# Seven quarter products for eight in the up and gate units of a two-block transformer kernel

## The chip, the cores and the metric

The kernel runs on one core of one Trainium2 chip. The metric is the device time of one execution in microseconds (us). An engine is called by its name in the profile: PE (matrix products; PEld are its weight loads), DVE (VectorE), ACT (ScalarE), POOL (GpSimd) and SP (which issues the weight transfers).

## The reference, cut to what matters

Two blocks in a row work on 512 tokens of 1024 features. The first has a gated feed-forward in each of its two layers, the second a squared-ReLU one in each of its two. These four are what the change touches:

```python
def swiglu_ffn(x, w_gate, w_up, w_down):                 # first block, 2 layers, D_FF = 2816
    return (jax.nn.silu(x @ w_gate) * (x @ w_up)) @ w_down
...
def sq_relu_mlp(h, w_up, w_down):                        # second block, 2 layers, D_FF_2 = 4096
    u = jax.nn.relu(h @ w_up)
    return (u * u) @ w_down
```

All else (an HGRN2 and convolution mixer, cross attention to 256 memory tokens, a pooling mixer, gated linear attention, sliding-window attention, norms) stays as it is.

## The kernel before, in words

**Precision.** Every float32 operand is split in two fp32r parts, a high one (a copy by ACT) and a low one (the rest, a subtraction by DVE), and each product is three matmuls: high by high, low by high, high by low (`mm3`).

**Units.** The weights come as 1 MB units of 128 x 2048 (w_raw, two slots, c % 2). Of unit c, ACT makes w_hi (`split_hi`), DVE makes w_lo (`split_lo`), and SP loads unit c + 2 into the slot when w_lo of unit c is there. ACT may write w_hi of unit c when PE has used unit c - 2 (semaphore unit_used).

**Chunks.** A feed-forward is cut in chunks of 256 hidden features: 11 for ffn0 and ffn1, 16 for mlp0 and mlp1. A chunk of an ffn has a gate unit, an up unit and a down unit, a chunk of an mlp an up and a down unit. An up or gate unit is 8 tiles of input features x 2 tiles of hidden features x 3 matmuls of 512 tokens, 48 in all, into two PSUM banks; a down unit is 8 output tiles x 2 x 3, also 48. The order in memory and on PE is up (gate, up) of chunk c + 1, then down of chunk c. The middle chunks run in hardware loops of two chunks a trip (`chunks` on each engine).

**Banks.** Banks 0 to 3 take the up and gate products, banks 4 to 7 the eight output tiles of a down unit, `4 + m % 4`. So the fifth tile (m = 4) needs the bank that DVE's `add` of the first has read, the sixth that of the second, the seventh (m = 6) that of the third, and so on.

**Work of DVE in a chunk of an mlp** (`up`, `down`): two products of a bank with rstd, two squared ReLUs, two rests (mhl), a w_lo of 2048 columns for each of the two units, and eight adds of the down tiles to the residual xs. ACT copies the hidden tiles (mhh) in between. In an ffn, ACT does the SiLU from the bank and DVE one product in place of the rstd and ReLU steps.

**Order.** Each engine's program is written out by hand and runs in that order; a wait on a semaphore holds up all that stands behind it on its engine.

## Time and profile before

| | before |
|---|---|
| device time, median of 3 runs | 2421.45 us (2421.07 to 2422.88) |
| span of the profiled execution | 2419.9 us |
| PE busy | 2386.0 us (99%) |
| DVE busy | 1448.5 us (60%) |
| ACT busy | 873.7 us (36%) |
| weights loaded | 204 issues of 1024 KB and a few smaller ones |

The profiled execution has no time of its own beside its span; the median of the runs is 1.55 us above that span. The spans of rows overlap: an instruction's duration on PE, DVE or ACT is longer than the distance to the next one, since the engines are pipelined. Where work follows without a wait, the distance from start to start is what it costs.

### The profile page before, as it was taken

Reading aid. Unit: us, or ns where it says so; the run is one execution under the profiler, and the core shown is the slowest. Engines: PE = TensorE matmul, PEld = TensorE weight load, DVE = VectorE, ACT = ScalarE, POOL = GpSimd, SP = SyncE. Lnnn points to the kernel's source line nnn. Section 1 sums busy time; section 2 is a strip of 40 time slices with the busy share of each in tenths; the row PEclk is TensorE's granted clock in tenths of the full one; section 3 lists DMA queues with packets and bytes.
Section 4 is the critical chain, followed back from the end, with each engine's and each line's share of the span. In section 5 each row is a group of like instructions: output and inputs, shape, how many; then the busy total and the mean of one; then the engine's idle time right before and its main releaser. Section 6 shows DMA issues by size and latency. Waiting matters only on the chain.

```text
span 2419.9 us, 28651 instructions
## 1 busy us (share of the span) xinstructions
PE 2386.0 (99%) x11134; PEld 1944.4 (80%) x11134; DVE 1448.5 (60%) x1994; ACT 873.7 (36%) x1230; POOL 22.7 (1%) x39
## 2 busy tenths in 40 slices
PE   8999999999999999999999999999999999999998
PEld 7887888888887887888887786888888777888886
DVE  6997646444446846444446725565566776665566
ACT  4455445222223834322223625422122465222122
POOL 0000000000000000000000000000000000000000
PEclk9999999999999999999999999999999999999999
DMA  5222312322222211222222220233333211222221
GB/s 183 105 101 92 122 35 105 114 104 88 103 88 103 77 64 70 105 97 94 97 94 102 77 105 35 83 109 118 120 112 120 87 53 64 93 96 95 104 90 66
DMA packets 38811, 228.06 MB, mean 94 GB/s; under 512 B 8837, under 2 KB 8917, under 8 KB 12496
## 3 DMA queue, kind: packets, MB, share of 16 engines
q1 hardware_dynamic: 31680, 219.17, 25.3%
q0 software_dynamic: 7056, 7.86, 1.3%
q8 instruction: 52, 0.85, 0.1%
q14 instruction: 23, 0.19, 0.0%
HBM read 221.71 MB, written 5.24 MB: 94 GB/s over the span
## 4 chain that ended last, share of the span: by engine, by line
PE 86%; DVE 7%; ACT 5%; issue 1%; DMA 1%; SPq 0%; DVEq 0%; ACTq 0%
PE bank L710 85%; DVE w_lo L2074 2%; ACT w_hi L1483 1%; DMA w_raw<-weights_in 1%; ACT xs L1564 1%; ACT xh L1502 1%; DVE xl L2089 1%; DVE cacc L2310 1%; PE bank L1414 1%; DVE xs L2204 0%; DVE xs L2184 0%; ACT pr L1806 0%; DVE sum_x L2096 0%; DVE sum_q L2103 0%; DVE xs L2160 0%
## 5 line engine op out<-in xcount | busy, mean ns | idle before, releaser
L2074 DVE TENSOR_TENSOR w_lo<-w_raw,w_hi 128x2048 fp32r<-128x2048 f32 x200 | 458.2, 2291 | 372.7 <-ACT w_hi L1483 372.6
L710 PE MATMUL bank<-xh,w_hi 128*128 128x512 f32 x1408 | 553.6, 393 | 13.3 <-DVE w_lo L2532 6.7
L710 PE MATMUL bank<-xl,w_hi 128*128 128x512 f32 x1408 | 548.9, 390 | 0.0
L710 PE MATMUL bank<-xh,w_lo 128*128 128x512 f32 x1408 | 548.8, 390 | 0.0
L1483 ACT ACTIVATE w_hi<-w_raw 128x2048 fp32r<-128x2048 f32 x200 | 381.6, 1908 | 400.1 <-PE bank L710 394.1
L2160 DVE TENSOR_TENSOR xs<-xs,bank 128x512 f32<-128x512 f32 x448 | 294.5, 684 | 102.1 <-PE bank L710 101.1
L710 PEld LDWEIGHTS bank<-xh,w_hi 128*128 128x128 f32 x1408 | 264.8, 188 | 77.2 <-DVE w_lo L2532 6.7
L710 PEld LDWEIGHTS bank<-xh,w_lo 128*128 128x128 f32 x1408 | 264.8, 188 | 55.4
L710 PEld LDWEIGHTS bank<-xl,w_hi 128*128 128x128 f32 x1408 | 265.0, 188 | 54.3 <-issue 0.5
L710 PE MATMUL bank<-yh,w_hi 128*128 128x512 f32 x576 | 227.2, 394 | 0.4 <-DVE w_lo L2074 0.3
L710 PE MATMUL bank<-yl,w_hi 128*128 128x512 f32 x576 | 224.3, 389 | 0.0
L710 PE MATMUL bank<-yh,w_lo 128*128 128x512 f32 x576 | 224.2, 389 | 0.0
L710 PE MATMUL bank<-mhh,w_hi 128*128 128x512 f32 x512 | 199.2, 389 | 0.0
L710 PE MATMUL bank<-mhl,w_hi 128*128 128x512 f32 x512 | 199.2, 389 | 0.0
L710 PE MATMUL bank<-mhh,w_lo 128*128 128x512 f32 x512 | 199.2, 389 | 0.0
L1622 ACT ACTIVATE mhh<-mh 128x512 fp32r<-128x512 f32 x64 | 39.5, 633 | 312.9 <-DVE mh L2254 312.9
L2249 DVE TENSOR_TENSOR mh<-bank,rstd 128x512 f32<-128x512 f32 x64 | 43.7, 691 | 173.8 <-PE bank L710 173.8
L710 PE MATMUL bank<-fhh,w_hi 128*128 128x512 f32 x352 | 136.9, 389 | 0.0
L710 PE MATMUL bank<-fhl,w_hi 128*128 128x512 f32 x352 | 136.9, 389 | 0.0
L710 PE MATMUL bank<-fhh,w_lo 128*128 128x512 f32 x352 | 136.9, 389 | 0.0
L710 PEld LDWEIGHTS bank<-yh,w_hi 128*128 128x128 f32 x576 | 108.1, 188 | 28.5 <-issue 6.6
L710 PEld LDWEIGHTS bank<-yh,w_lo 128*128 128x128 f32 x576 | 108.1, 188 | 22.9
(299 smaller groups left out, 2868.3 us busy)
## 6 DMA issues: line engine op xcount, KB each, us to landing
w_raw<-weights_in SPq DMA_DIRECT2D x204, 1024.0 KB, 4.8
rel_scratch<-vt POOLq DMA_DIRECT2D x8, 384.0 KB, 19.9
bias<-rel_scratch POOLq DMA_DIRECT2D x8, 256.0 KB, 3.2
y_out<-xs SPq DMA_DIRECT2D x8, 256.0 KB, 2.2
xs<-x_in SPq DMA_DIRECT2D x3, 512.0 KB, 8.7
mk<-mem_in POOLq DMA_DIRECT2D x1, 1024.0 KB, 7.3
window<-consts_in POOLq DMA_DIRECT2D x1, 576.0 KB, 6.4
xs<-x_in SPq DMA_DIRECT2D x2, 256.0 KB, 4.5
```

What stands on the lines that cost most here:

```text
L710: return pe.matmul(dst, a, b, start=start, stop=stop)
L1414: last = pe.transpose(bank(key)[:, s_ * P:(s_ + 1) * P], pv[:, s_ * P:(s_ + 1) * P], ident[:, :])
L1483: act.activation(w_hi[:, slot(c), :], w_raw[:, c % 2, :], ACT.Copy).then_inc(w_hi_ready, 1)
L1502: give(act.activation((xh if dst is None else dst)[:, k, :], src, ACT.Copy, **kw), "x_hi")
L1564: give(act.activation(xs[:, k, :], xs[:, k, :], ACT.Identity, scale=col(f"{param}_g{l}", k), bias=col(f"{param}_b{l}", k)), "xn_ready")
L1622: give(act.activation(hh[:, chunk % 2, m, :], src, ACT.Copy), "hh_ready")
L2074: dve.tensor_tensor(w_lo[:, slot(c), :], w_raw[:, c % 2, :], w_hi[:, slot(c), :].bitcast(F32), ALU.subtract)\
L2089: return dve.tensor_tensor(l, src, h, ALU.subtract)
L2160: free(dve.tensor_tensor(xs[:, k, :], xs[:, k, :], bank(key)[:, :], ALU.add), key)
L2249: free(dve.tensor_tensor(hid[:, chunk % 2, m, :], bank(key)[:, :], rstd[:, :], ALU.mult), key)
L2310: ins = dve.scalar_tensor_tensor(a, u, wj, a, ALU.mult, ALU.add)
```

## The change

In all up and gate units but the first of each ffn stage (gate 0 and up 0) and the first two up units of each mlp, the product of 1024 inputs x 256 features with 512 tokens is split in quarters (512 inputs, 128 features, 256 tokens) and made of seven quarter products where eight would be plain (Strassen's scheme in its form with 15 sums). That is 10 gate and 10 up units in each ffn, 14 up units in each mlp, 68 in all. A quarter product is 4 tiles x 3 = 12 matmuls of 256 tokens, a unit 84 of them.

What this needs beside the products:

- four combinations of quarters of the input (tf, split to th and tl), made once for each of the four stages on DVE and ACT (`combined_sums`, `combined_hi`, `combined_lo`);
- four combinations of the quarters of each unit's weights (`quad_sums` on DVE; one is written over a quarter of w_raw), three of them split beside the unit (hix by ACT, lox by DVE: 1536 columns more than the 2048);
- the seven products share three banks: P1, P2, P3 add up in one, Q1 and Q2 lie in halves of bank 2, R in bank 3. ACT copies out partial results of 256 columns (`partial`, into rb), DVE adds them up (`tile_sum`), and the hidden steps read SBUF in place of a bank;
- w_hi and w_lo are made in pieces of 1024 columns, and DVE's list for a chunk is written anew (`beside_up`, `beside_down`, `beside_gate`, `plain_hidden`);
- th, tl, tf and the rest take SBUF from memh and meml, the split memory tokens. POOL stores these two (1 MB each) to DRAM when they are made and loads them back when the last up unit of ffn0 is used; PE waits for that (mem_back) ahead of the memory values of the second layer. The loads of the bias table (8 issues) start at the last up unit of mlp0 and not spread over its last twelve units.

```diff
+                def seven(tag, which, c, i=None, first=False):
...
+                    def product(f, dst, w_, x_, start=False):
+                        for k in range(4):
+                            a = slice(k * P, (k + 1) * P)
+                            last = mm3(dst, (w_[0][:, a], w_[1][:, a]), x_(k), start and k == 0, k == 3, shared=True)
+                        if f:
+                            full(last, (name, tag, which, f))
...
+                    p_, q_, r_ = (bank((name, tag, which, f)) for f in ("P1", "Q1", "R"))
+                    at_piece(1)
+                    free_bank("P1")
+                    product("P1", p_[:, 0:MEM], of_unit(0), quarter(0, 0), start=True)
+                    free_bank("Q1")
+                    product(None, q_[:, 0:MEM], of_unit(1), quarter(1, 0), start=True)
+                    at_piece(2)
...
+                    product("Q1", q_[:, MEM:], of_sums(0), combined(0))
...
+                    free_bank("P2")
+                    product("P2", p_[:, 0:MEM], of_sums(1), combined(1))
+                    at_piece(3)
+                    free_bank("R")
+                    product("R", r_[:, 0:MEM], of_unit(3), combined(2), start=True)
+                    pe.wait_ge(w_lo_ready, at(i, per, c + 1))
+                    free_bank("Q2")
+                    product("Q2", q_[:, MEM:], of_sums(2), quarter(1, 1))
+                    free_bank("P3")
+                    product("P3", p_[:, 0:MEM], of_unit(2), combined(3))
...
+                def gated_step(tag, c, i=None):
+                    seven(tag, "u", up_unit(name, c), i)
+                    down(tag, down_unit(name, c - 1), c - 1, i)
+                    seven(tag, "g", gate_unit(name, c + 1), i)
...
+                def plain_step(tag, c, i=None, first=False):
+                    down(tag, down_unit(name, c), c, i)
+                    seven(tag, "u", up_unit(name, c + 2), i, first)
```

On DVE, in the mlp (the gated list is the same, with one product `fh * sil` for each tile in place of `plain_hidden`, and the sums of the next up unit ahead of the last three adds):

```diff
+            def plain_hidden(tag, chunk, i=None):
+
+                key = (name, tag, "u")
+                for m in range(2):
+                    h = mh[:, chunk % 2, m, :]
+                    wait_drained(dve, (*key, "P3" if m else "Q2"), i)
+                    dve.scalar_tensor_tensor(h, h, 0.0, rstd[:, :], ALU.max, ALU.mult).then_inc(sem["hf_step"], 1)
+                for m in range(2):
...
+                    dve.tensor_tensor(h, h, h, ALU.mult).then_inc(sem["hf_ready"], 1)
...
+            def beside_down(tag, n, chunk, i=None, after=None):
+
+                quad(n, 0, i)
+                adds(tag, (0,), i)
+                quad(n, 1, i)
+                rests(chunk, 0, i)
+                adds(tag, (1,), i)
+                quad(n, 2, i)
+                rests(chunk, 1, i)
+                adds(tag, (2,), i)
+                quad(n, 3, i)
+                adds(tag, (3, 4), i)
+                if after is not None:
+                    sums_of(after, i)
+                adds(tag, (5, 6, 7), i)
...
+            def plain_step(tag, c, i=None, after=True):
+                beside_down(tag, up_unit(name, c + 2), c + 1, i)
+                beside_up(tag, c + 2, down_unit(name, c + 1), c % 2, up_unit(name, c + 3) if after else None, i)
+                plain_hidden(tag, c + 2, i)
...
                 if gate:
+                    combined_sums()
+                    sums_of(gate_unit(name, 1))
+                    if name == "ffn0":
+                        dve.wait_ge(mem_stored, 2 * 16)
+                    combined_lo()
+                    scale_residual()
+                    for piece in range(4):
+                        quad(gate_unit(name, 1), piece)
...
                 else:
+                    split_lo(U + 1)
+                    combined_sums()
+                    combined_lo()
+                    first_hidden("p0", 0)
+                    split_lo(U + 2)
+                    sums_of(up_unit(name, 2))
+                    for m in range(2):
+                        rests(0, m)
+                    first_hidden("p1", 1)
```

**DVE in the loop of mlp0, from where PE has ended an up unit.** Here stood the two bank drains, two ReLUs and two rests (mhl), then two adds, the w_lo of the next up unit in one piece, and more adds (rows of register arithmetic stand between):

```order
L2249 TENSOR_TENSOR mh<-bank,rstd 128x512 x2
L2254 SCALAR_TENSOR_TENSOR mh<-mh 128x512
L606 REGISTER_ALU
L2254 SCALAR_TENSOR_TENSOR mh<-mh 128x512
L2257 REGISTER_ALU
L2258 TENSOR_TENSOR mhl<-mh,mhh 128x512
L2257 REGISTER_ALU
L2258 TENSOR_TENSOR mhl<-mh,mhh 128x512
L593 REGISTER_ALU
L2160 TENSOR_TENSOR xs<-xs,bank 128x512
L593 REGISTER_ALU
L2160 TENSOR_TENSOR xs<-xs,bank 128x512
```

In the changed kernel the same place has, after the last tile_sum and the hidden steps, the pieces of the next up unit ahead of and between the adds:

```order
L2579 TENSOR_TENSOR mh<-rb,bank 128x512
L2665 SCALAR_TENSOR_TENSOR mh<-mh,rstd 128x512
L679 REGISTER_ALU
L2665 SCALAR_TENSOR_TENSOR mh<-mh,rstd 128x512
L2668 REGISTER_ALU
L2669 TENSOR_TENSOR mh<-mh 128x512
L2668 REGISTER_ALU
L2669 TENSOR_TENSOR mh<-mh 128x512
L2532 REGISTER_ALU
L2537 TENSOR_TENSOR w_lo<-w_raw,w_hi 128x1024
L666 REGISTER_ALU
L2437 TENSOR_TENSOR xs<-xs,bank 128x512
```

The first add stood behind six instructions of 512 columns; it now stands behind five of 512 (from the last tile_sum on) and one of 1024. In `beside_down` two more of 1024, two rests and two adds come before the third.

**DVE ahead of the first down unit of mlp0.** These rows, from the w_lo of the second up unit on, stand in the changed kernel; before, the two bank drains followed that w_lo at once:

```order
L2351 TENSOR_TENSOR w_lo<-w_raw,w_hi 128x2048
L2611 TENSOR_SCALAR ngain<-prm 128x4
L2620 SCALAR_TENSOR_TENSOR tf_y<-xs,ngain,half_y 128x256 x4
L2620 SCALAR_TENSOR_TENSOR tf_y<-xs,prm,half_y 128x256 x4
L2620 SCALAR_TENSOR_TENSOR tf_y<-xs,prm,tf_y 128x256 x8
L2636 TENSOR_TENSOR tl_y<-tf_y,th_y 128x1024 x4
L2676 SCALAR_TENSOR_TENSOR mh<-bank,rstd 128x512 x2
L2680 TENSOR_TENSOR mh<-mh 128x512 x2
L2351 TENSOR_TENSOR w_lo<-w_raw,w_hi 128x2048
```

All the combinations of the input now lie between the second up unit's w_lo and the first chunk's hidden steps, for whose rests the first down unit waits.

## Rows read from the trace of the kernel before

**Rows 1.** The page: PE's busy time, and its granted clock in 40 slices

```profile
PE 2386.0 (99%) x11134; PEld 1944.4 (80%) x11134; DVE 1448.5 (60%) x1994; ACT 873.7 (36%) x1230; POOL 22.7 (1%) x39
PEclk9999999999999999999999999999999999999999
```

**Rows 2.** Windows: mlp0 from its first down unit; busy (x instructions)

```profile
1580.66:1907.00 326.34, 326.34 (x1441) 270.08 (x1439) 205.83 (x251) 78.04 (x65) 14.35 (x16) 1.00 0.35 113
```

**Rows 3.** Timeline of PE: start, duration; 12 matmuls of 512 columns apart

```profile
600.19 0.39 PE L710 MATMUL bank<-xh,w_hi 128*128 128x512 f32 x1
...
602.91 0.39 PE L710 MATMUL bank<-xh,w_hi 128*128 128x512 f32 x1
```

**Rows 4.** Timeline of PE: matmuls of 256 columns, 46 apart

```profile
145.40 0.28 PE L710 MATMUL bank<-meml,w_hi 128*128 128x256 f32 x1
...
150.92 0.28 PE L710 MATMUL bank<-memh,w_lo 128*128 128x256 f32 x1
```

**Rows 5.** Timeline of DVE, one chunk of mlp0

```profile
1732.50 1.37 DVE L2249 TENSOR_TENSOR mh<-bank,rstd 128x512 f32<-128x512 f32 x2 [5.96 <-PE bank L710]
...
1737.58 2.29 DVE L2074 TENSOR_TENSOR w_lo<-w_raw,w_hi 128x2048 fp32r<-128x2048 f32 x1
1739.79 2.48 DVE L2160 TENSOR_TENSOR xs<-xs,bank 128x512 f32<-128x512 f32 x4
```

**Rows 6.** Timeline of DVE: 1024 columns; and 512 with a column of prm as scalar

```profile
1323.96 1.22 DVE L2081 TENSOR_TENSOR glr_lo<-w_raw,glr_hi 128x1024 fp32r<-128x1024 f32 x1
...
1332.57 0.75 DVE L2090 SCALAR_TENSOR_TENSOR xl<-xs,prm,xh 128x512 fp32r<-128x512 f32 x1
1333.23 0.69 DVE L2204 TENSOR_TENSOR xs<-xs,rstd 128x512 f32<-128x512 f32 x1
```

**Rows 7.** Timeline: PE passes to the next unit, ACT and then DVE follow

```profile
696.75 0.39 PE L710 MATMUL bank<-xh,w_hi 128*128 128x512 f32 x1
696.95 1.92 ACT L1483 ACTIVATE w_hi<-w_raw 128x2048 fp32r<-128x2048 f32 x1 [7.71 <-PE bank L710]
698.90 2.29 DVE L2074 TENSOR_TENSOR w_lo<-w_raw,w_hi 128x2048 fp32r<-128x2048 f32 x1 [1.27 <-ACT w_hi L1483]
```

**Rows 8.** The page, costliest groups: ACT at 2048 and 512 columns (mean ns)

```profile
L1483 ACT ACTIVATE w_hi<-w_raw 128x2048 fp32r<-128x2048 f32 x200 | 381.6, 1908 | 400.1 <-PE bank L710 394.1
L1622 ACT ACTIVATE mhh<-mh 128x512 fp32r<-128x512 f32 x64 | 39.5, 633 | 312.9 <-DVE mh L2254 312.9
```

**Rows 9.** Timeline, ffn1: DVE's w_lo of up unit 0, PE behind it, the scalings

```profile
970.10 2.29 DVE L2074 TENSOR_TENSOR w_lo<-w_raw,w_hi 128x2048 fp32r<-128x2048 f32 x1
...
972.77 0.40 PE L710 MATMUL bank<-xl,w_hi 128*128 128x512 f32 x1
...
976.59 2.77 DVE L2224 TENSOR_SCALAR xs<-xs 128x512 f32<-128x512 f32 x8
```

**Rows 10.** Timeline, mlp0: the drain behind w_lo of the second up unit; first down

```profile
1569.34 1.27 DVE L2249 TENSOR_TENSOR mh<-bank,rstd 128x512 f32<-128x512 f32 x2
...
1580.66 0.39 PE L710 MATMUL bank<-mhh,w_hi 128*128 128x512 f32 x1
```

**Rows 11.** Timeline of PE at the start of the program

```profile
10.30 0.63 PE L710 MATMUL bank<-xh,w_lo 128*128 128x512 f32 x1
10.73 0.63 PE L710 MATMUL bank<-xh,w_hi 128*128 128x512 f32 x1
```

**Rows 12.** The page, DMA issues: KB each, median us to landing

```profile
w_raw<-weights_in SPq DMA_DIRECT2D x204, 1024.0 KB, 4.8
...
bias<-rel_scratch POOLq DMA_DIRECT2D x8, 256.0 KB, 3.2
...
mk<-mem_in POOLq DMA_DIRECT2D x1, 1024.0 KB, 7.3
```

**Rows 13.** Timeline of PE: the first matmul after a wait, and the next

```profile
790.75 0.39 PE L710 MATMUL bank<-w_hi,xh 128*128 128x256 f32 x1 [0.48 <-DVE w_lo L2074]
790.97 0.28 PE L710 MATMUL bank<-w_lo,xh 128*128 128x256 f32 x1
```

More of the change, by code:

```diff
@@ new lines, in chunks, with up @@
+                sums = 4 if gate else 2
+                per = 6 if gate else 4
+                def up(tag, which, c, ready=None):
+                    pe.wait_ge(w_lo_ready, c + 1)
+                    for m in range(2):
+                        wait_free(pe, (name, tag, which, m))
+                    for k in range(KT):
+                        if ready:
+                            ready(k)
+                        for m in range(2):
+                            last = mm3(bank((name, tag, which, m))[:, :], weights(c, k * 256 + m * P, P), src(k),
+                                       k == 0, k == KT - 1)
+                            if k == KT - 1:
+                                full(last, (name, tag, which, m))
@@ L1638, in chunks, with half_hi @@
-                if not gate:
-                    up("late", c, 2 * trips + 1)
-                    down(c + k_)
-                    c += k_ + 1
-                down(c)
+                th, tf = (th_x, tf_x) if gate else (th_y, tf_y)
+                units, sums = (6, 4) if gate else (4, 2)
+                def half_hi(c, piece, i=None):
+                    half = UNIT // 2
+                    a = slice(piece * half, (piece + 1) * half)
+                    if piece == 0:
+                        act.wait_ge(raw_loaded[c % 2], at(i, 8 * units, 16 * (c // 2 + 1)))
+                        act.wait_ge(unit_used, at(i, units, c - 1))
+                    ins = act.activation(w_hi[:, slot(c), a], w_raw[:, c % 2, a], ACT.Copy)
+                    if piece == 1:
+                        ins.then_inc(w_hi_ready, 1)
@@ new lines, in quad, with partial, silu @@
+                def quad(c, piece, i=None):
+                    quads_hi(c, piece, i, units, sums)
+                def partial(tag, which, f, par, i=None):
+                    key = (name, tag, which, f)
+                    to = {"P1": 0, "P2": 1, "R": 2, "Q1": 3}[f]
+                    wait_full(act, key, i)
+                    free(act.activation(rb[:, par, to, :], half_bank(key), ACT.Copy), key)
+                def silu(tag, c, m, i=None):
+                    wait_drained(act, (name, tag, "g", "P3" if m else "Q2"), i)
+                    give(act.activation(sil[:, m, :], sil[:, m, :], ACT.Silu), "sil_ready")
@@ new lines, in hidden, with combined_hi @@
+                def hidden(chunk, m, i=None):
+                    if gate and chunk == 0:
+                        wait_drained(act, (name, "p0", "u", m))
+                    else:
+                        act.wait_ge(sem["hf_ready"], at(i, 4, hf_base[name] + 2 * chunk + m + 1))
+                    h = hid[:, m, :] if gate else hid[:, chunk % 2, m, :]
+                    give(act.activation(hh[:, chunk % 2, m, :], h, ACT.Copy), "hh_ready")
+                def combined_hi():
+                    for j in (0, 3, 1, 2):
+                        seen.next("t_ready")
+                        give(act.activation(th[:, j, :, :].rearrange("p k t -> p (k t)"), tf[:, j, :], ACT.Copy), "t_hi")
@@ L2242, in up, with first_hidden @@
+                def first_hidden(tag, chunk):
                     for m in range(2):
                         key = (name, tag, "u", m)
[L2244 to L2249 removed]
@@ L2274, in chunks @@
-                c += trips * per
-                if not gate:
-                    up("late", c, 2 * trips + 1)
-                    down("late", c + k_)
-                    c += k_ + 1
+                        wait_full(dve, key)
+                        free(dve.scalar_tensor_tensor(mh[:, chunk % 2, m, :], bank(key)[:, :], 0.0, rstd[:, :], ALU.max, ALU.mult), key)
+                    for m in range(2):
+                        h = mh[:, chunk % 2, m, :]
+                        wait_drained(dve, (name, tag, "u", m))
+                        dve.tensor_tensor(h, h, h, ALU.mult).then_inc(sem["hf_ready"], 1)
@@ L2279, in chunks @@
+                adds(tag, (0,))
+                half_lo(down, 0)
+                adds(tag, (1,))
+                half_lo(down, 1)
+                for m in range(2):
+                    rests(last_chunk, m)
+                adds(tag, range(2, KT))
+                c = down
                 keys = last_down_keys(name)
```

556 lines of the change are left out of this document (419 added, 137 removed).

## The prediction

> **What bounds the kernel now.** I read the page first. PE is busy for 2386.0 of 2419.9 us and its granted clock stands at 9 in all 40 slices [rows 1]: what is on PE's path is nearly all of the time, and what other engines do costs something only when PE waits for it. The windows say the same of the stage: mlp0 from its first down unit has PE busy in all of its 326.34 us, DVE in 205.83 [rows 2]. A unit's price is then read from starts, since durations overlap: twelve matmuls of 512 columns lie 2.72 us apart, 0.2267 each [rows 3], so a unit of 48 takes 10.88 us. A chunk of an mlp is two units (21.76 us), of an ffn three (32.64 us). The other view that matters is DVE's timeline, because DVE frees the banks of the down tiles.
>
> **Gain on PE.** 256 columns cost 0.1200 each (5.52 us over 46) [rows 4]. A unit of 84 takes 10.08 us and saves 0.80, not an eighth (1.36): between 512 and 256 columns half of 0.2267 would be 0.1133, and 0.007 is left on each matmul. 68 units save 54.4 us. The trace has this shape with weights and inputs in the same precision, so this term is safe as long as PE never waits. The Trainium skill's page "TensorE: Matmul & The Clock Gate" (Back-to-back issue gap) gives N / 2.4 + 2.5 ns for the isolated gap: 109.2 and 215.8 ns, by which a unit would save 1.19 us and the change 81 us. The rows have 120 and 227 ns, and the sum goes by the rows.
>
> **Prices on DVE and ACT.** DVE, starts of instructions that follow at once: 512 columns 0.60 (four adds: 2.48 less the last one's 0.69, over three), 2048 columns 2.21 (1737.58 to 1739.79) [rows 5]. 1024 columns last 1.22 [rows 6]; less the 0.085 by which a duration exceeds a distance (0.69 against 0.60, 2.29 against 2.21) that is 1.137. 512 columns with a column of prm cost 0.66 [rows 6]; a 256 one is taken at 0.40 (half of 0.53 streaming, 0.07 fixed, 0.06 for prm); it has no row, the bounds are 0.33 and 0.46. ACT: 1908 ns for 2048 and 633 for 512 columns [rows 8], so 1.06 for 1024 and 0.42 for 256. Hand-offs: PE's next unit starts at 696.75, ACT at 696.95: 0.20. ACT ends at 698.87, DVE starts at 698.90: 0.03 [rows 7]. DVE to PE: w_lo ends at 972.39 and the second matmul stands at 972.77, one distance behind a first at 972.54 [rows 9]: 0.15, and a first matmul after a wait costs 0.10 more than a next one, 0.22 [rows 13] against 0.12. I take 0.20 from DVE's end to PE's effective start; bounds 0.10 and 0.30.
>
> **A chunk of an mlp afterwards.** DVE's work per chunk, in columns: 8 adds, 2 tile sums, 4 hidden steps, 2 rests, 4 weight sums (20 x 0.60 = 12.0), five pieces of 1024 (5.7), one of 512 (0.6) and about 0.1 for a sum that waits for its forerunner: 18.4 us of 20.96. It fits, but its order decides. Let the up unit end at 0. DVE can do its last tile sum from 0.20; then two steps with rstd, two squares, a piece, add 0, a piece, rest, add 1, a piece, rest, add 2. Up to the end of add 1 that is 8 x 0.60 + 2 x 1.137 = 7.1, and PE can start the sixth tile at 0.20 + 7.1 + 0.085 + 0.20 = 7.6; it would come there at 5 x 1.36 = 6.80: PE waits 0.8. Up to the end of add 2 it is 10 x 0.603 + 3 x 1.137 = 9.44, and PE can start the seventh tile at 9.93, against 8.16: 1.77 in all, the first 0.8 within it. Nothing of this can run ahead: the last tile sum needs P3, the hidden steps are behind it, the pieces and the adds behind those. ACT does not bind (first piece by 1.3, hidden copies right behind their squares). The seventh and eighth tile and the seven products follow: 9.93 + 2.72 + 10.08 = 22.73 us a chunk against 21.76 before. **The steady chunk is 0.97 slower, though PE's work in it is 0.80 shorter.** It is a closed ring: the next up unit ends 22.73 later and the ring starts anew. Per mlp 13 down units pay 1.77 and the first and last about 0.65 each (there DVE has less to do ahead): 24.3.
>
> **A chunk of an ffn afterwards.** The same ring with two products in place of four hidden steps: 8 x 0.603 + 3 x 1.137 + 0.20 + 0.285 = 8.72 against 8.16: PE waits 0.57. Sixth tile: 6.4 against 6.80, no wait. Step 21.53 + 10.08 = 31.6 against 32.64. Nine of them per ffn: 5.1 us. The two seven-product units that follow each other (gate, up) do not wait: ACT's pieces (3.7 us for unit and sums) and four copies at 0.42 go into 10.08, and the tile sum of Q2, the last thing needed, is there 0.9 after P3 begins, where its bank is wanted 2.9 after.
>
> **Lead-ins.** These have no cover. In mlp0, DVE is free from 1569.34 and PE starts the first down unit at 1580.66 [rows 10]. In between, the change puts: 16 products of 256 (6.34) and ngain (0.1), four lows of 1024 (4.55), four hidden steps (2.4), w_lo of the down unit (2.2), weight sums (2.5), two rests (1.2), and 0.1 of waiting: 19.4. PE starts at 1569.34 + 19.4 + 0.29 = 1589.0: 8.4 late. Before, the same stretch had 4 x 0.60 + 2 x 0.60. In ffn1, DVE is free at 972.3 and PE ends up unit 0 at 972.54 + 10.88 = 983.4 [rows 9]. The change puts four combinations (4.7), weight sums (2.5), four lows (4.55), eight scalings (2.77 less 0.085) and the first piece (1.14): 15.6, PE starts at 988.1: 4.7 late. Then P1 takes 1.44, and the next product needs bank 2, which DVE drains three pieces and one product later (3.5 + 0.28): 2.0 more. Per ffn 6.7.
>
> **POOL and transfers.** memh and meml go out and back, 1 MB each; a megabyte took 7.3 us, so about 15 us [rows 12]. They come back while two down units (21.8 us) and the norm run. The eight bias loads at 3.2 each (26 us) start two down units ahead of the end of mlp0, and the key unit and the first query unit (16 us on PE) lie between that end and their reader. Weight loads take 4.8 of every 10.9 us. All at nothing; without cover I would see 5 to 10 us.
>
> **Sum.** mlp: 2 x (8.4 + 24.3 - 14 x 0.80) = +43.0. ffn: 2 x (6.7 + 5.1 - 20 x 0.80) = -8.4. Together +34.6. Against the profiled execution's 2419.9 us span that is 2454.5, and with the 1.55 us by which the median stands above it, **2456**.
>
> **Rivals.**
> - *DVE comes in time in the loops.* The point is in the ring: were the seventh tile's chain 1.77 us shorter in the mlp (9.93 to 8.16; three of its ten short instructions), the 24.3 and 5.1 per stage would vanish: -54.4 + 2 x 8.4 + 2 x 6.7 = -24, 2397 us, faster. It would take DVE instructions at 0.46 and not 0.60, or a down unit that waits later than I read. Against: eight adds in a row of the trace keep 0.60. Half that shortening gives about 2423. With hidden lead-ins too, 2367. Chance 0.15, and 0.04 for what lies within 0.2% of before.
> - *Waits cost PE even when they are met.* An up unit before had three waits at its start; seven products have ten spread over them. Should each product pay the 0.10 of [rows 13], 68 x 7 x 0.10 = 48 us come on top where DVE does not hide it (in the ring of the mlp it is on the path too): 2485 to 2505. Against: [rows 2] hold 16 down units with eight bank waits each and the 326.34 us over 1440 matmuls are 0.2266, so a met wait costs nothing at 512 columns; at 256 the unit has 0.10 less room for each. Chance 0.10.
> - *The clock falls in the lead-ins.* PE would stand for 8.4 us; in the kernel before its idle time is 33.9 us in all, the first load included [rows 1], in many short pieces. At the start, cold, 512 columns cost 0.43 [rows 11], the lower of the two levels (1.2 GHz). If four lead-ins cost ten such matmuls, 0.2 each, that is up to 8 us: 2464; the mlp's ring takes up part of it. The Trainium skill (same page, The HAM clock gate) says that the default state is throttled and that activity releases it, which speaks for this; no row here shows a fall. It stays within the range and the forecast's chance.
> - *The change doesn't do what it says:* excluded, since the listing of PE's program has 84 matmuls of 256 columns in each such unit.
>
> **Numbers.** Forecast with its own spread (hand-off 0.10 to 0.30: 56 stalls, -5 to +6; 256-wide products: +-2; a dependent step that waits 0.1 more in each ring: +5; clock: +8): 2446 to 2475, chance 0.69. Faster 0.16 (the first rival and 0.01), within 0.2% (4.8 us, about what a measurement can tell from no change) 0.04, slower 0.80, of it 0.10 for the costly waits. The range leaves out most of the faster cases and the upper end of the costly ones: 2425 to 2490.
>
> **What the profile after would show.** Matmuls of 256 columns 0.120 apart; PE idle about 1.8 us in each down unit of the mlps at its sixth and seventh tile, ended by DVE's add of xs; 0.6 in those of the ffns; 8.4 us ahead of the first down unit of each mlp, ended by DVE's mhl, and 4.7 and 2.0 in front of the first seven products of an ffn. mlp0 from its first down unit would take about 339 us and not 326. The prediction is wrong if PE has no idle in the down units (then it is faster), or if starts of 256-column matmuls lie wider than 0.12.

## The result, and the profile after

| | before | after |
|---|---|---|
| device time, median of 4 runs each | 2421.96 us (2421.07 to 2422.88) | 2465.77 us (2463.97 to 2466.8) |
| ratio, 95% interval | | 1.0179, 1.0164 to 1.0193 |
| span of the profiled execution | 2419.9 us | 2462.2 us |

Slower by 43.8 us; the forecast was 2456, in a range of 2425 to 2490. On the page after, PE is busy for 20.1 us less than in [rows 1] and DVE for 406 us more than in the table of before, and DVE has 19% of the chain that ended last:

```profile
PE 2365.9 (96%) x13582; PEld 2019.4 (82%) x13582; DVE 1854.8 (75%) x2716; ACT 1106.8 (45%) x1782; POOL 24.8 (1%) x43
...
PE 67%; DVE 19%; issue 8%; ACT 4%; DMA 1%; DVEq 1%; SPq 0%; ACTq 0%
```

PE's waits after (engine, line, who ended it: us in total, times, longest):

```profile
PE bank L804 <- DVE xs L2437: 37.7, 74, 0.7
PE bank L804 <- DVE mhl L2587: 16.8, 2, 8.4
PE bank L804 <- DVE w_lo L2537: 9.0, 2, 4.5
...
PE bank L804 <- DVE fh L2727: 1.1, 2, 0.5
```

The first row is the ring of the down units, the others are the lead-ins. A wait's figure is idle time only; a wait in the ring costs 0.27 to 0.29 us more than it says (worked out from the distances below), and the page counts that part as busy. That explains most of why PE is busy for only 20.1 us less and not for the 54.4 us of the gain: some 80 waits at 0.28 are 22 us, and the slow matmuls behind the lead-ins, shown below, some 7 (an estimate from these rows).

**One chunk of mlp0, PE's timeline after** (start, duration, then the wait and its releaser). The sixth and the seventh tile of a down unit start at 1637.40 and 1639.73; then the change from 512 to 256 columns:

```profile
1636.50 0.39 PE L804 MATMUL bank<-mhh,w_lo 128*128 128x512 f32 x1
1637.40 0.50 PE L804 MATMUL bank<-mhh,w_hi 128*128 128x512 f32 x1 [0.52 <-DVE xs L2437]
1637.74 0.39 PE L804 MATMUL bank<-mhl,w_hi 128*128 128x512 f32 x1
...
1638.66 0.40 PE L804 MATMUL bank<-mhh,w_lo 128*128 128x512 f32 x1
1639.73 0.51 PE L804 MATMUL bank<-mhh,w_hi 128*128 128x512 f32 x1 [0.67 <-DVE xs L2437]
1640.08 0.40 PE L804 MATMUL bank<-mhl,w_hi 128*128 128x512 f32 x1
...
1642.59 0.28 PE L804 MATMUL bank<-yh,w_hi 128*128 128x256 f32 x1
1642.70 0.28 PE L804 MATMUL bank<-yl,w_hi 128*128 128x256 f32 x1
1642.82 0.28 PE L804 MATMUL bank<-yh,w_lo 128*128 128x256 f32 x1
```

The distances over the two waits are 0.90 and 1.07 us and not 0.23, and the matmul behind each comes 0.34 or 0.35 later: 0.79 and 0.96 us are lost. The 256-column products lie 0.12 apart, as in [rows 4]. The DVE rows of the same chunk show what the wait is for:

```profile
1630.18 0.69 DVE L2579 TENSOR_TENSOR mh<-rb,bank 128x512 f32<-128x512 f32 x1 [0.84 <-PE bank L804]
1630.79 1.28 DVE L2665 SCALAR_TENSOR_TENSOR mh<-mh,rstd 128x512 f32<-128x512 f32 x2
1631.99 1.28 DVE L2669 TENSOR_TENSOR mh<-mh 128x512 f32<-128x512 f32 x2
1633.20 1.22 DVE L2537 TENSOR_TENSOR w_lo<-w_raw,w_hi 128x1024 fp32r<-128x1024 f32 x1
1634.33 0.68 DVE L2437 TENSOR_TENSOR xs<-xs,bank 128x512 f32<-128x512 f32 x1
1634.93 1.21 DVE L2540 TENSOR_TENSOR lox_y<-ext_y,hix_y 128x1024 fp32r<-128x1024 f32 x1
1636.07 0.68 DVE L2587 TENSOR_TENSOR mhl<-mh,mhh 128x512 fp32r<-128x512 f32 x1
1636.67 0.68 DVE L2437 TENSOR_TENSOR xs<-xs,bank 128x512 f32<-128x512 f32 x1
1637.27 1.22 DVE L2537 TENSOR_TENSOR w_lo<-w_raw,w_hi 128x1024 fp32r<-128x1024 f32 x1
```

The last tile sum starts when P3 is done (1630.18, a wait for PE), and the second add of xs ends at 1637.35, 0.05 ahead of PE's restart. No instruction between them waits: this is the ring. The downs of four chunks start 22.77 us apart (1607.13, 1629.89, 1652.66, 1675.43).

**The lead-in of mlp0.** PE's rows answer to [rows 10]. The windows below them (length, then busy time and count of PE, PEld, DVE, ACT and POOL, then the granted clock, DMA's share and GB/s) are those behind the lead-ins of mlp0 (the first two), mlp1 and ffn1:

```profile
1575.81 0.39 PE L804 MATMUL bank<-yh,w_lo 128*128 128x512 f32 x1
1584.63 0.79 PE L804 MATMUL bank<-mhh,w_hi 128*128 128x512 f32 x1 [8.44 <-DVE mhl L2587]
1585.22 0.63 PE L804 MATMUL bank<-mhl,w_hi 128*128 128x512 f32 x1
1585.65 0.63 PE L804 MATMUL bank<-mhh,w_lo 128*128 128x512 f32 x1
```

```profile
1580.66:1587.60 6.94, 2.96 (x7) 2.42 (x8) 6.91 (x12) 2.32 (x3) 0.00 (x0) 0.51 0.46 151
1587.60:1595.00 7.40, 7.40 (x33) 6.08 (x33) 7.40 (x11) 1.35 (x3) 0.00 (x0) 1.00 0.00 0
...
2107.65:2113.20 5.55, 5.55 (x13) 4.38 (x14) 5.55 (x8) 2.62 (x4) 0.00 (x0) 0.50 0.06 27
...
985.10:993.70 8.60, 8.04 (x36) 7.75 (x37) 8.56 (x12) 3.46 (x5) 0.00 (x0) 0.50 0.37 124
```

After 8.4 us without a product the granted clock is at its lower level (1.2 GHz), and the first seven matmuls lie 0.43 apart, as at the start of the program [rows 11]; later they lie 0.23 apart. In mlp1 it is 13 matmuls. The Trainium skill ("TensorE: Matmul & The Clock Gate", The HAM clock gate) calls the throttled state the default one that activity releases; these windows agree.

**The lead-in of ffn0**, PE:

```profile
440.94 0.58 PE L804 MATMUL bank<-xh,w_hi 128*128 128x256 f32 x1 [4.50 <-DVE w_lo L2537]
441.32 0.42 PE L804 MATMUL bank<-xl,w_hi 128*128 128x256 f32 x1
441.54 0.42 PE L804 MATMUL bank<-xh,w_lo 128*128 128x256 f32 x1
...
444.42 0.39 PE L804 MATMUL bank<-xh,w_hi 128*128 128x256 f32 x1 [0.54 <-DVE fh L2727]
```

P1's twelve matmuls stand 0.214 apart and not 0.120, and the wait for bank 2 behind them is short. In ffn1 the waits are 4.48 and 0.54, and there 24 more matmuls behind bank 2 stand 0.214 apart; in ffn0 only the twelve do.

**Where the time went, by stage.** Starts of the first and the last down matmul of each stage, and what lies between; forecast are the terms of the prediction's sum, put to the same stretches:

| stretch | before | after | difference | forecast |
|---|---|---|---|---|
| start to ffn0's first down | 457.39 | 463.22 | +5.8 | +5.1 |
| ffn0, first to last down | 315.29 | 306.37 | -8.9 | -9.3 |
| to ffn1's first down | 232.55 | 240.05 | +7.5 | +5.1 |
| ffn1, first to last down | 315.29 | 306.45 | -8.8 | -9.3 |
| to mlp0's first down | 260.13 | 268.55 | +8.4 | +8.4 |
| mlp0, first to last down | 326.17 | 340.51 | +14.3 | +13.1 |
| to mlp1's first down | 174.05 | 182.50 | +8.5 | +8.4 |
| mlp1, first to last down | 326.17 | 341.73 | +15.6 | +13.1 |

With the tail (-0.1) that is +42.3, the difference of the spans; the forecast's terms are +34.6.

### The profile page after: what moved, and what is told of

It reads as the page before. It is cut to its first block, busy times and chain, and to the rows that moved or that the text cites. A ratio compares the mean times of both kernels' runs of the same rounds, so it can differ in the third digit from the quotient of the medians.

```text
span 2462.2 us, 36009 instructions
## 1 busy us (share of the span) xinstructions
PE 2365.9 (96%) x13582; PEld 2019.4 (82%) x13582; DVE 1854.8 (75%) x2716; ACT 1106.8 (45%) x1782; POOL 24.8 (1%) x43
## 4 chain that ended last, share of the span: by engine, by line
PE 67%; DVE 19%; issue 8%; ACT 4%; DMA 1%; DVEq 1%; SPq 0%; ACTq 0%
PE bank L804 66%; DVE w_lo L2537 3%; DVE xs L2437 3%; DVE w_lo L2351 2%; DVE mhl L2587 2%; ACT w_hi L1651 1%; DVE mh L2669 1%; ACT xh L1670 1%; ACT xs L1732 1%; DMA w_raw<-weights_in 1%; DVE fhl L2587 1%; DVE tf_y L2620 1%; DVE xl L2366 1%; DVE cacc L2797 1%; DVE lox_x L2540 1%
## 5 line engine op out<-in xcount | busy, mean ns | idle before, releaser
L804 PE MATMUL bank<-xh,w_hi 128*128 128x512 f32 (+1 forms) x1088 | 397.9, 366 | 22.9 <-DVE w_lo L2537 9.0
L804 PE MATMUL bank<-xh,w_lo 128*128 128x512 f32 (+1 forms) x1088 | 392.5, 361 | 0.0
L804 PE MATMUL bank<-xl,w_hi 128*128 128x512 f32 (+1 forms) x1088 | 392.5, 361 | 0.0
L2437 DVE TENSOR_TENSOR xs<-xs,bank 128x512 f32<-128x512 f32 x448 | 292.3, 679 | 37.7 <-PE bank L804 34.3
L2351 DVE TENSOR_TENSOR w_lo<-w_raw,w_hi 128x2048 fp32r<-128x2048 f32 x80 | 183.1, 2289 | 129.8 <-ACT w_hi L1651 129.7
L2564 DVE TENSOR_TENSOR w_lo<-w_raw,w_hi 128x1024 fp32r<-128x1024 f32 x104 | 123.0, 1220 | 116.2 <-ACT w_hi L1798 116.2
L1798 ACT ACTIVATE w_hi<-w_raw 128x1024 fp32r<-128x1024 f32 x104 | 108.9, 1051 | 222.2 <-PE bank L804 222.2
L1810 ACT ACTIVATE rb<-bank 128x256 f32<-128x256 f32 x272 | 103.9, 382 | 218.9 <-PE bank L804 216.8
L1651 ACT ACTIVATE w_hi<-w_raw 128x2048 fp32r<-128x2048 f32 x80 | 152.5, 1906 | 79.3 <-PE bank L804 71.5
L1775 ACT ACTIVATE w_hi<-w_raw 128x1024 fp32r<-128x1024 f32 x68 | 72.1, 1061 | 235.8 <-PE bank L804 235.8
L2537 DVE TENSOR_TENSOR w_lo<-w_raw,w_hi 128x1024 fp32r<-128x1024 f32 x136 | 165.6, 1218 | 7.6 <-ACT w_hi L1780 7.5
L804 PEld LDWEIGHTS bank<-mhh,w_hi 128*128 128x128 f32 x512 | 97.2, 190 | 89.9 <-DVE xs L2437 54.5
L804 PE MATMUL bank<-yh,w_hi 128*128 128x256 f32 (+1 forms) x352 | 116.2, 330 | 0.2 <-DVE w_lo L2351 0.2
```

The costliest lines, as they stand in the source:

```text
L804: return pe.matmul(dst, a, b, start=start, stop=stop, skip_group_check=shared)
L1651: act.activation(w_hi[:, slot(c), :], w_raw[:, c % 2, :], ACT.Copy).then_inc(w_hi_ready, 1)
L1775: act.activation(w_hi[:, s_, 0:half], w_raw[:, c % 2, 0:half], ACT.Copy).then_inc(sem["hi_piece"], 1)
L1798: ins = act.activation(w_hi[:, slot(c), a], w_raw[:, c % 2, a], ACT.Copy)
L1810: free(act.activation(rb[:, par, to, :], half_bank(key), ACT.Copy), key)
L2351: dve.tensor_tensor(w_lo[:, slot(c), :], w_raw[:, c % 2, :], w_hi[:, slot(c), :].bitcast(F32), ALU.subtract)\
```

## Experiments

Each was timed beside the kernel before on the same chip (its medians there: 2421.41 to 2422.57 us); differences from the changed kernel or between experiments are differences of medians taken at different times, so a few tenths of a microsecond mean nothing. The theory is that DVE's list is a closed ring behind each up unit, and that the four lead-ins, with the clock that falls in them, do the rest. Its rivals: transfers cost something, waits cost PE even when met, or DVE simply has too much to do in a chunk, in whatever order.

### Adds first

In `beside_down`, one list for mlp and ffn:

```diff
-                    quad(n, 0, i)
-                    adds(tag, (0,), i)
-                    quad(n, 1, i)
-                    rests(chunk, 0, i)
-                    adds(tag, (1,), i)
-                    quad(n, 2, i)
-                    rests(chunk, 1, i)
-                    adds(tag, (2,), i)
-                    quad(n, 3, i)
-                    adds(tag, (3, 4), i)
+                    adds(tag, (0, 1, 2), i)
+                    quad(n, 0, i)
+                    adds(tag, (3,), i)
+                    quad(n, 1, i)
+                    rests(chunk, 0, i)
+                    adds(tag, (4,), i)
+                    quad(n, 2, i)
+                    rests(chunk, 1, i)
+                    quad(n, 3, i)
```

> The changed kernel with one list rewritten: in the down units DVE does the adds of tiles 0, 1 and 2 first and only then the pieces of the next unit and the rests, the same work in another order. Ring theory (the wait in the down units is DVE's order, not its load): add 2 is done 5.3 us after the up unit's end against 8.16 wanted, so the stalls of 1.8 us in each down unit of the mlps and 0.6 in the ffns vanish; only the lead-ins (2 x 8.4 + 2 x 6.7) and some 6 us of lower clock stay. 58 us less than the changed kernel: about 2405 us, faster than before. Rival (met waits cost PE, or DVE's load as such): no change from 2466 beyond 10 us.

Measured: 2408.24 us (2407.89 to 2408.58), ratio 0.9944 (0.9929 to 0.9959). The same instructions in another order take 57.5 us less. PE's waits of this kernel:

```profile
PE bank L804 <- DVE mhl L2587: 16.9, 2, 8.4
PE bank L804 <- DVE w_lo L2537: 9.0, 2, 4.5
...
PE bank L804 <- DVE xs L2437: 1.9, 4, 0.7
```

The waits for xs went from 37.7 to 1.9 us, the lead-ins stay as they were. mlp0 from first to last down takes 318.35 us, PE busy for 318.08 of it, DVE for 278.56:

```profile
1573.63:1891.98 318.35, 318.08 (x1944) 286.85 (x1944) 278.56 (x387) 121.29 (x176) 14.36 (x16) 0.99 0.36 116
```

So DVE's load (88% of the stretch) fits, and its order was what cost. The rival of costly met waits falls too: it asks for 0.7 us more in each unit, 9.8 in this stretch, but a chunk now takes 20.98 us, and its matmuls alone 10.88 + 10.08 = 20.96. From 326.17 the 14 units should take 11.2 and take 7.8; of the missing 3.4 some 2.4 are twelve matmuls at half clock behind the lead-in:

```profile
1573.63:1578.80 5.17, 5.17 (x12) 4.11 (x13) 2.96 (x5) 2.62 (x4) 0.00 (x0) 0.50 0.06 24
```

### One more DVE instruction, in the ring and beside it

The kernel after with a sum that nobody reads, in one kernel ahead of `beside_down` (in the ring), in the other between `beside_down` and `beside_up`:

```diff
 def plain_step(tag, c, i=None, after=True):
+    dve.tensor_tensor(mean[:, :], rstd[:, :], rstd[:, :], ALU.add)
     beside_down(tag, up_unit(name, c + 2), c + 1, i)
```

> The changed kernel with one unneeded DVE instruction of 512 columns (0.60 us) in each mlp chunk between the squares and the first piece, that is in the ring. Ring theory: all 28 chunks get 0.6 longer, +16.8 us, about 2482. Rival (PE or its waits bound the chunk, DVE has time): no change, 2466.

> The same unneeded instruction in each mlp chunk, placed behind the eight adds, where DVE has slack while PE does the seven products. Ring theory: 0 to +1 us, 2466. Rival (DVE's whole load bounds the chunk, 18.4 us of work): +16.8, as with the instruction in the ring.

Measured: in the ring 2481.33 us (2480.29 to 2483.18), beside it 2465.59 us (2464.8 to 2466.84). The same instruction costs 15.7 us more in one place than in the other. It runs 28 times. By the traces a chunk of the mlps takes 23.37 us with it in the ring and 22.77 with it beside the ring, as without it, from the second down unit on: 0.60 in each of 26 chunks, which makes 15.6. The first down unit of each mlp, which starts at the lower clock, does not show it, so the 16.8 us of the expectation were not reached. In the ring DVE's time is PE's time, one for one; behind the eight adds it costs nothing.

### The transfers alone

The kernel before, with POOL's two stores and two loads of the memory halves, PE's wait for them, and the bias loads at the end of mlp0:

```diff
+            for part, a in enumerate((memh, meml)):
+                pool.dma_start(mem_kept[part, :, :, :], a[:, :, :].bitcast(F32)).then_inc(mem_stored, 16)
...
+            pool.wait_ge(unit_used, UNITS["ffn0"] + 31)
+            pool.wait_ge(mem_stored, 2 * 16)
+            for part, a in enumerate((memh, meml)):
+                pool.dma_start(a[:, :, :].bitcast(F32), mem_kept[part, :, :, :]).then_inc(mem_back, 16)
```

> The kernel before with only the transfers of the change: memh and meml stored to DRAM and loaded back behind the last up unit of ffn0 with PE's wait on them, and the eight bias loads started at the last up unit of mlp0. Forecast of the prediction: nothing, within 1 us of 2421.5. Rival (not hidden): 5 to 10 us slower.

Measured: 2422.44 us against 2422.36 beside it, ratio 1.0001 (0.9992 to 1.001). In the kernel before they cost nothing that can be told from noise, and the rival's 5 to 10 us are out.

### The array kept busy in the lead-ins

The kernel after, with products that nobody reads (30 in each mlp's lead-in, 16 in each ffn's) into a bank that is free then:

```diff
+            def busy_until(key, a, n):
+                wait_free(pe, key)
+                for _ in range(n):
+                    mm(bank(key)[:, :], a[:, 0, 0:P], a[:, 0, :], True, True)
...
                     up("p0", "u", U + 1)
+                    busy_until((name, 0, "d", 3), xh, 16)
...
                     up("p1", "u", U + 1)
+                    busy_until((name, 0, "d", 3), yh, 30)
```

> The changed kernel with unneeded matmuls of 512 columns into a free bank in the four lead-ins: 30 (6.8 us) ahead of the first down unit of each mlp, 16 (3.6 us) ahead of the first seven products of each ffn. They end before the wait does. Theory (some 7 us of the 9.7 by which the result lies above the forecast are the lower clock behind the lead-ins): the granted clock stays whole and the time falls by 5 to 7 us, to about 2460. Rival (the rest comes from waits or the transfers): no change, 2465.8, at a full clock or not.

Measured: 2461.12 us (2460.33 to 2461.61), 4.65 less than the changed kernel. Around the starts of both mlps' down units the granted clock now is at full height throughout:

```profile
1580.00:1590.00 10.00, 8.36 (x38) 6.58 (x37) 9.96 (x14) 4.31 (x6) 0.00 (x0) 1.00 0.31 105
2095.00:2112.00 17.00, 15.39 (x69) 12.41 (x68) 16.96 (x22) 8.06 (x10) 0.00 (x0) 1.00 0.19 64
```

mlp0 and mlp1 from first to last down take 339.7 us both, against 340.5 and 341.7, and the forecast's 339.3. So 2.8 of the 3.7 us of excess over the forecast in these two stretches were the clock.

In the ffns the same run shows something else. P1 now runs at full clock, and the wait for bank 2 behind it, 0.54 us before, is 1.8, near the forecast's 2.0:

```profile
PE bank L804 <- DVE fh L2735: 3.6, 2, 1.8
...
446.00:452.00 6.00, 6.00 (x44) 6.00 (x43) 5.96 (x8) 4.15 (x8) 0.00 (x0) 0.81 0.29 119
989.90:995.00 5.10, 5.09 (x30) 5.09 (x31) 5.07 (x8) 3.90 (x7) 0.00 (x0) 0.67 0.61 206
```

So the slow P1 had cost nothing: bank 2 is free no sooner. But the granted clock now falls behind this wait, and 17 matmuls stand 0.214 apart in each ffn. Against the trace of the changed kernel, where only ffn1 had slow matmuls behind bank 2, that gives 0.6 us back ahead of ffn1's first down unit and loses 1.2 ahead of ffn0's. The spans of the two profiled executions differ by 2.4 us and not by 4.65; the profiled execution of the changed kernel is the shortest of its four.

### The lead-in of the mlp, and that of the ffn

Both on the kernel with the adds first. mlp: two more up units are plain, so that the combinations are first needed two down units later and are made while PE works (ACT's list is rewritten to match):

```diff
-_units = [up_unit(_name, c) for c in range(2, MLP_CHUNKS)]
+_units = [up_unit(_name, c) for c in range(4, MLP_CHUNKS)]
...
                     split_lo(U + 1)
-                    combined_sums()
-                    combined_lo()
                     first_hidden("p0", 0)
                     split_lo(U + 2)
-                    sums_of(up_unit(name, 2))
                     for m in range(2):
                         rests(0, m)
+                    combined_sums()
                     first_hidden("p1", 1)
```

> The kernel with the adds first, and in the mlps four plain up units and not two, the combinations of the input made beside the first two down units, behind the first chunk's hidden steps and rests. Lead-in theory: the waits of 8.6 us and the lower clock behind them (about 2 us each) go, 2 x 2 x 0.80 of PE work comes back: -17 us against 2408.2, about 2391. Rival (the wait only moves to the first seven products, since DVE has as much to do): 2400 or more.

Measured: 2390.85 us (2387.62 to 2392.35), 17.4 less than with the adds first alone; PE's wait for mhl is gone.

ffn: the first pieces of the weights and the products of the plain units come ahead of three of the four lows, and the scalings of the residual last (the lists of PE and ACT are rewritten to match):

```diff
-                    combined_lo()
-                    scale_residual()
-                    for piece in range(4):
-                        quad(gate_unit(name, 1), piece)
+                    quad(gate_unit(name, 1), 0)
+                    quad(gate_unit(name, 1), 1)
+                    combined_lo((0,))
...
+                    combined_lo((3, 1, 2))
```

> The kernel with the adds first, and in the ffns the first two pieces of gate unit 1 and the two products that drain banks 2 and 3 ahead of three of the four input lows, the scaling of the residual behind it all. No work is removed. Lead-in theory: the waits of 4.7 and 2.0 us in each ffn and the lower clock go: -13 to -16 us against 2408.2, about 2394. Rival (DVE's load up to the first down unit binds, some 35 us in 31): it gives back half, about 2401.

Measured: 2392.6 us (2390.08 to 2393.26), 15.6 less. PE's wait for w_lo of L2537 is gone.

> All three rewritings together. If the parts add up: 2408.2 - 17 - 14 = 2377 us, 1.8% faster than the kernel before; PE then waits nowhere in the feed-forwards for over 1 us, and what is left of the 54.4 us of gain is 54.4 less 3.2 (four fewer such units).

Measured: 2381.98 us, ratio 0.984 (0.9823 to 0.9856), but its four runs lie at 2376.83, 2378.77, 2385.24 and 2385.19. By the sum of both gains it would be 2375.2; only the lower two come within 4 us of that.

### What the scatter of 8 us is

The trace of the kernel with both lead-ins mended, taken from the fastest of its four runs, has something in mlp0 that mlp1 has not. PE waits 1.83 us for xs at 1642.28 and 0.6 us later runs at the lower clock for a few matmuls, and DVE had waited at 1635.40 for a weight load:

```profile
1635.40 0.69 DVE L2540 TENSOR_TENSOR ext_y<-w_raw 128x512 f32<-128x512 f32 x1 [5.30 <-DMA w_raw<-weights_in]
```

In mlp0 alone POOL stores the bias table (rel_scratch, 8 stores of 384 KB), one each 21 us. From 1620 to 1642 us the weight loads beside such a store land after 9.3 us (count, KB, median us to landing), against 4.7 in mlp1 (2120 to 2142):

```profile
w_raw<-weights_in SPq DMA_DIRECT2D x2, 1024.0 KB, 9.3
rel_scratch<-vt POOLq DMA_DIRECT2D x1, 384.0 KB, 19.2
```

The kernel before has these stores and these late loads too; nothing there waits for them. From 1600 to 1730 us of its trace:

```profile
w_raw<-weights_in SPq DMA_DIRECT2D x12, 1024.0 KB, 9.9
```

In eight traces of this case with all eight stores (before, changed, adds first, the mlp's lead-in, and the four with both lead-ins), the landing goes with how far behind a store the weight load is issued. Within 0.5 us of the store, ahead of it or behind, it takes 5.2 to 6.2 us (kernels with the adds first and the lead-ins as they were or mended); 0.7 us behind it 9.4 (twice); 1.6 to 7.1 us behind it 8.7 to 13.4. The load that the weight sums of DVE wait for stands at most 0.5 us from the store in most chunks here, but 0.7 behind it at 1625.9, the one of the wait above. No run changed this distance alone.

Four runs go at this. The same kernel again, and one whose stores are issued one unit earlier (`UNITS["mlp0"] + 2 + 2 * g` for `+ 3 + 2 * g`):

> The kernel with both lead-ins mended, but POOL issues each of its eight stores of the bias table in mlp0 (384 KB, 19 us to landing) one unit earlier, so that it goes beside the other weight load of a chunk. In the run with both lead-ins mended the fourth store stood at 1625.20 and the weight load of the next up unit was waited for by DVE's weight sums for 5.3 us; PE then waited 1.83 us in the down unit and had 3.4 us at half of its clock. Theory A (the store delays the load that is needed first): no such wait of over 3 us on w_raw in mlp0, mlp0 from first to last down unit 317.6 us as mlp1 has it (321.4 in that run), time 2373 to 2377 and runs within 3 us of each other. Rival B (the late load is chance, and so is the scatter between 2376.8 and 2385.2 us): runs scatter by 8 us here as well, median 2377 to 2382. Rival C (the other load is then late): wait of DVE on w_raw by ACT's w_hi, mlp0 slower than 321.4, 2380 or more.

> The kernel with both lead-ins mended once more, unchanged, beside the one with the stores a unit earlier. Its four earlier runs gave 2376.8, 2378.8, 2385.2 and 2385.2 us. By theory A (stores of the bias table delay a weight load in mlp0 by an amount that differs from run to run) the scatter comes again, 2376 to 2386, and is wider than that of the kernel with the stores a unit earlier. By rival B both scatter alike.

Measured: with the stores a unit earlier 2389.02 us (2386.55 to 2392.58), again as it was 2384.92 (2378.17 to 2386.56, five runs, with the same 8 us between them). My expectation of a gain had the wrong sign. The rival C came in its time, but mostly not in its place (a wait at ACT's copy): the load that DVE's weight sums wait for now stands 11 to 16 us behind a store and lands after 7.5 to 11.1 us in all six chunks from 1600 to 1730, where it took 5.3 to 5.9 in most of them before. It is the sums that wait longer; ACT's copies wait for loads 10.1 us in all, 10.7 before. DVE's waits for w_raw in mlp0, first as it was (again), then a unit earlier:

```profile
DVE ext_y L2540 <- DMA w_raw<-weights_in: 19.7, 10, 9.5
```

```profile
DVE ext_y L2540 <- DMA w_raw<-weights_in: 33.4, 11, 6.4
```

The wait of 9.5 us is followed on PE by 6.65 us without a product, and by the lower clock:

```profile
1664.60 0.39 PE L808 MATMUL bank<-mhh,w_lo 128*128 128x512 f32 x1
1671.64 0.79 PE L808 MATMUL bank<-mhh,w_hi 128*128 128x512 f32 x1 [6.65 <-DVE xs L2459]
1672.23 0.63 PE L808 MATMUL bank<-mhl,w_hi 128*128 128x512 f32 x1
```

mlp0 takes 329.6 us there and mlp1 317.7. The last two runs go at the cause in two ways. One leaves out seven of the eight stores; the loads of the bias table all read the one that is left, so the table is wrong for 14 of the 16 heads and with it the output:

```diff
                 pool.wait_ge(unit_used, UNITS["mlp0"] + 3 + 2 * g)
-                pool.dma_start(scratch[heads, :, :], vt[heads, 0:384].unsqueeze(1).broadcast_to([2, P, 384])).then_inc(vec_stored, 16)
-            pool.wait_ge(vec_stored, 8 * 16)
+                if g == 0:
+                    pool.dma_start(scratch[heads, :, :], vt[heads, 0:384].unsqueeze(1).broadcast_to([2, P, 384])).then_inc(vec_stored, 16)
+            pool.wait_ge(vec_stored, 16)
...
-                shifted = bass.AP(tensor=scratch.tensor, offset=2 * g * P * 384 + 127, ap=[[383, P], [P * 384, 2], [1, 2 * P]])
+                shifted = bass.AP(tensor=scratch.tensor, offset=127, ap=[[383, P], [P * 384, 2], [1, 2 * P]])
```

> The kernel with both lead-ins mended, with the first of the eight stores of the bias table alone; the other seven are left out, and the loads of the bias table read the first pair of heads for all, so the table is wrong for 14 of the 16 heads. Theory A (the stores delay weight loads in mlp0): DVE waits for w_raw in mlp0 no longer than in mlp1 (5.0 us in 11 waits, 1.8 the longest), no wait of PE for xs there, mlp0 takes 317.6 us, time 2373 to 2376, runs within 3 us of each other. Rival B (chance in the weight loads themselves): the scatter of 8 us and single waits of 5 to 9 us stay.

Measured: 2375.09 us, five runs from 2374.83 to 2375.34. The scatter of 8 us is 0.5 now, the weight loads from 1600 to 1730 us land after 4.7 us at the median, and both mlps take the same:

```profile
1551.26:1868.92 317.66, 317.39 (x1873) 282.77 (x1871) 276.36 (x379) 118.35 (x164) 6.90 (x9) 1.00 0.32 107
2042.82:2360.51 317.69, 317.42 (x1873) 282.77 (x1871) 275.32 (x380) 116.79 (x165) 0.00 (x0) 1.00 0.26 90
```

The other keeps all stores and lets DVE meet the late load behind the adds 0 to 2:

```diff
                     adds(tag, (0, 1, 2), i)
+                    if not gate:
+                        sums_of(n, i)
```

(and no longer in `beside_up`).

> The kernel with both lead-ins mended, with DVE's four weight sums of an mlp's up unit moved from ahead of the tile sums of the unit before to behind the adds 0 to 2. What a late weight load holds up is then no longer the tile sums, the hidden steps and the adds that PE waits for: the sums stand some 7 us later in the ring, and PE needs what comes of them from 12 us on. By my count DVE's fourth add ends 9.3 us behind the up unit and PE wants its bank at 9.5, so nothing should wait otherwise. Theory A (late loads of w_raw beside the stores of the bias table hold up the adds): PE's waits for xs in mlp0 (8.7 us in the last run) go, mlp0 takes 317.6 us as mlp1, time 2373 to 2377, runs within 3 us. Rival B (the scatter has another source): runs still scatter by 8 us. Rival C (the sums are now too late for the first products that use them): PE waits for lox in the up units, slower than 2385.

Measured: 2382.03 us (2381.63 to 2383.96), ratio 0.9837 (0.9824 to 0.9851). The scatter is 2.3 us, but the level is not the forecast's 2373 to 2377. DVE's and PE's waits in mlp0:

```profile
PE bank L808 <- DVE xs L2459: 5.4, 7, 1.2
...
DVE ext_y L2540 <- DMA w_raw<-weights_in: 5.6, 6, 1.2
```

The sums now stand ahead of the fourth add, which by my count had 0.2 us to spare; DVE waits 5.6 us for loads and PE 5.4 for xs, about 1 us in a chunk. The loads now go out 2.0 to 2.8 us behind the stores and land after 12.7 to 13.0 us, every one of them, which fits the steadier and slower level. mlp0 takes 325.1 us, mlp1, without the stores, 319.1 against 317.7 with the sums ahead. The long waits are gone, short ones have come: neither order is immune to a load that lands late.

## Why the prediction came out as it did

- **Gain on PE, 54.4 us: right.** 0.12 a matmul in the sevens; with the ring open (adds first) a chunk takes 20.98 us for 21.76, 0.78 less where the term says 0.80. mlp0 shrinks by 7.8 us, and by the term's 11.2 but for 1 us once the clock's part is taken out.
- **The ring of the mlp: right.** Forecast 22.73 us a chunk, measured 22.77. PE loses 0.79 at the sixth tile and 0.96 at the seventh, 1.75 for the 1.77 forecast. The extra instruction in and beside the ring shows the mechanism and not only the size; the other order of the same list shows that it is the order.
- **The ring of the ffn: right within 0.5 us a stage** (-8.9 and -8.8 for -9.3).
- **Lead-ins of the mlps: right**, 8.4 forecast, 8.44 and 8.40 waited.
- **Lead-in of the ffns: right for the path, short by the clock.** 4.7 forecast, 4.50 and 4.48 waited. Then 2.0 were forecast at bank 2, and 0.54 waited: P1 ran at the lower clock and took 12 x 0.214 = 2.57 us in place of 1.44, which filled part of the wait. With the array kept busy P1 ran at full clock and 1.8 were waited, so the term was read rightly. The stretch as a whole is 0.7 (ffn0) and 2.4 us (ffn1) over the forecast.
- **Transfers at nothing: right** (ratio 1.0001 on the kernel before).
- **What was mis-sized: the term for the clock.** The prediction left it out of the sum and gave it up to 8 us as a rival. The sum fell short of the difference of spans by 42.3 - 34.6 = 7.7 us. In mlp0 and mlp1 7 and 13 matmuls at 0.43 for 0.23 make 1.4 and 2.6 us, against an excess of 1.2 and 2.5 there. In ffn1 the lower clock lasts from 985.1 to 993.7; its 24 matmuls behind bank 2 make 2.2, against an excess of 2.4. These three excesses are 6.1 of the 7.7, the slow matmuls in them 6.2. The remaining 1.6 (0.4 to 0.7 in each of the ffns' other stretches) was not tracked further. Another 2 us of the 9.8 between 2456 and 2465.77 is in no stretch of the table: the median lies 3.6 us above the profiled span after, and the prediction took the 1.55 of before. The profiled execution is the shortest of four, whose spans are 2462.2 to 2465.0 us at granted clocks of 0.993 (the two shorter) and 0.991 (the two longer), so part of these 2 us is likely the clock too; one trace alone does not show it.
- **The rival that DVE comes in time** gave 2397 for order made harmless; the kernel with adds first took 2408.24, lead-ins with their clock included. Its condition was counted loosely: the chain of 9.44 us must be 7.67, for which the ten short instructions would take 0.43 each, or all thirteen be faster by a fifth (0.49); 0.46 is neither. DVE kept 0.60, so nothing hangs on it.

## What to carry to other kernels

When products are made cheaper by sums on another engine (here DVE), add up that engine's list between the event that feeds it and the event that PE waits for, not its busy share: the same list, 88% busy, was harmless in one order and cost 57.5 us in another. Put first what frees a bank, then what prepares the next unit. Work ahead of the loop had no cover here and was paid twice, in its length and in a clock that had fallen; and a schedule tightened this far is exposed to transfers that were free before.

## What the runs showed of the hardware that was not expected

- A store of 384 KB in short packets (under 512 B: 1948 of the 2920 between 1600 and 1660 us in the kernel with both lead-ins) raises the landing of 1 MB weight loads beside it from 4.7 to 8.9 and 9.3 us at the median, and single ones to 13.4: in the kernel run again DVE stood 9.48 us for that one. How late differs from run to run, and with it the time, by 8 us. The kernel without seven of the stores shows that they are the cause (2374.8 to 2375.3 against 2376.8 to 2386.6). Which loads suffer goes with their distance from the store (5.2 to 6.2 us within 0.5 us of it, 9.4 at 0.7, up to 13.4 beyond); why it does, and whether the short packets matter, no run shows.
- The granted clock fell after 4.5, 6.65 and 8.4 us without a product, and once behind a wait of only 1.83 us in a down unit of the kernel with both lead-ins mended (mean 0.58 from 1642.28 to 1646.30); with the array kept busy it fell behind the waits of 1.8 us for bank 2 in both ffns. Behind twelve slow matmuls and a wait of 0.54 us it was back in ffn0, and stayed low for 24 matmuls of 256 columns more in ffn1. It came back after 7 matmuls of 512 columns in mlp0 and after 13 in mlp1, behind waits of the same length.
- The best kernels here that compute the whole reference are those with the adds first and both lead-ins mended: with the sums ahead of the adds nine runs from 2376.8 to 2386.6 us, median 2384.9 (1.5% under the kernel before), with the sums behind them five runs at a median of 2382.0 (1.6%).
